# A four-layer transformer block in fp32 parts on one core: a reciprocal, three copies, key parts and an output product change places in the latent-attention layers

## What is computed

```python
h = x @ w_in
cq, ckv, k_rope, gate = split(h)              # 384, 256, 32 and 1024 columns
q  = (rmsnorm(cq, q_norm) @ w_q_up)           # 16 heads of 64 + 32
kv = (rmsnorm(ckv, kv_norm) @ w_kv_up)        # 16 heads of 64 (key) + 64 (value)
q_rope, k_rope = rope(q[..., 64:]), rope(k_rope)      # one rotary key for all heads
s = (q_full @ k_full.T) * scale; causal mask; p = softmax(s)
y = ((p @ v) * silu(gate)) @ w_out
x = layernorm(ALPHA * x + y)
```

## Time and profile before

| | us |
|---|---|
| median of three runs (1685.38 to 1687.06) | 1685.86 |
| the profiled execution's own time | 1687.21 |
| its span, first to last instruction | 1685.4 |
| TensorE busy | 1653.2 (98%) |
| VectorE busy | 775.5 (46%) |
| ScalarE busy | 768.0 (46%) |
| GpSimd busy | 657.7 (39%) |

### The profile page before, as it was taken

The page is one execution under the profiler, slowest core; times in us unless marked ns, Lnnn a source line. Parts: engine busy times, 40 slices in busy tenths (PEclk is TensorE's granted clock), DMA queues, the critical chain, the costliest instruction groups (busy, mean ns, idle before and its releaser), DMA issues.

```text
span 1685.4 us, 24539 instructions
## 1 busy us (share of the span) xinstructions
PE 1653.2 (98%) x9349; PEld 1344.0 (80%) x9349; DVE 775.5 (46%) x2038; ACT 768.0 (46%) x1565; POOL 657.7 (39%) x551
## 2 busy tenths in 40 slices
PE   8999999999999999999999999999999999999998
PEld 8777779777888787778777778777788888888877
DVE  2777636566343434336777636888142111001052
ACT  4566724566243535534566635336753222222252
POOL 4423224332243423234322224792154444444423
PEclk9999999999999999999999999999999999999999
DMA  6322144323442222153223145432153333333422
GB/s 171 70 45 73 50 160 133 78 65 61 153 146 76 78 62 79 47 176 108 62 45 84 47 154 143 129 88 76 41 171 102 100 93 95 100 100 88 125 63 88
DMA packets 216048, 161.19 MB, mean 96 GB/s; under 512 B 53755, under 2 KB 197147, under 8 KB 215932
## 3 DMA queue, kind: packets, MB, share of 16 engines
q1 hardware_dynamic: 205904, 130.21, 27.6%
q10 hardware_dynamic: 9804, 29.38, 5.6%
q0 software_dynamic: 224, 0.03, 0.1%
HBM read 148.32 MB, written 11.14 MB: 95 GB/s over the span
## 4 chain that ended last, share of the span: by engine, by line
PE 85%; DVE 6%; ACT 6%; issue 1%; POOL 1%; DMA 0%; ACTq 0%; DVEq 0%; SPq 0%; POOLq 0%
PE banks L481 23%; PE banks L483 22%; PE banks L482 22%; PE banks L740 5%; PE banks L701 4%; PE banks L755 4%; ACT AB L1487 1%; PE banks L906 1%; PE banks L724 1%; ACT w_hi L1357 1%; ACT G L1616 1%; DVE AB L2231 1%; ACT AB L1513 1%; PE banks L714 1%; POOL w_lo L2828 0%
## 5 line engine op out<-in xcount | busy, mean ns | idle before, releaser
L2828 POOL TENSOR_TENSOR w_lo<-w_raw,w_hi 128x512 fp32r<-128x512 f32 (+2 forms) x506 | 617.0, 1246 | 998.4 <-ACT w_hi L1357 987.2
L481 PE MATMUL banks<-XTh,w_hi 128*128 128x512 f32 (+5 forms) x1216 | 451.7, 371 | 2.6 <-DVE XTl L2290 1.4
L483 PE MATMUL banks<-XTh,w_lo 128*128 128x512 f32 (+5 forms) x1216 | 444.3, 365 | 0.0
L482 PE MATMUL banks<-XTl,w_hi 128*128 128x512 f32 (+5 forms) x1216 | 444.3, 365 | 0.0
L1357 ACT ACTIVATE w_hi<-w_raw 128x1024 fp32r<-128x1024 f32 (+4 forms) x254 | 250.3, 996 | 157.8 <-PE banks L483 106.4
L481 PEld LDWEIGHTS banks<-XTh,w_hi 128*128 128x128 f32 (+2 forms) x1216 | 228.1, 188 | 45.6 <-issue 5.2
L483 PEld LDWEIGHTS banks<-XTh,w_lo 128*128 128x128 f32 (+2 forms) x1216 | 228.0, 188 | 38.2
L482 PEld LDWEIGHTS banks<-XTl,w_hi 128*128 128x128 f32 (+2 forms) x1216 | 228.3, 188 | 37.2 <-issue 1.2
L481 PE MATMUL banks<-w_hi,OTh 128*128 128x512 f32 (+1 forms) x448 | 173.0, 386 | 0.6 <-DVE QKl L2055 0.5
L483 PE MATMUL banks<-w_hi,OTl 128*128 128x512 f32 (+1 forms) x448 | 167.9, 375 | 0.0
L482 PE MATMUL banks<-w_lo,OTh 128*128 128x512 f32 (+1 forms) x448 | 167.9, 375 | 0.0
(11 more groups left out here) (212 smaller groups left out, 2333.7 us busy)
## 6 DMA issues: line engine op xcount, KB each, us to landing
w_raw<-in_w_gate_up_dram SPq DMA_DIRECT2D x44, 512.0 KB, 3.8
w_raw<-in_fox_w_in_dram SPq DMA_DIRECT2D x30, 512.0 KB, 4.1
w_raw<-in_mla_w_in_dram SPq DMA_DIRECT2D x26, 512.0 KB, 4.7
w_raw<-in_w_in_dram SPq DMA_DIRECT2D x24, 512.0 KB, 3.9
w_raw<-in_w_down_dram SPq DMA_DIRECT2D x22, 512.0 KB, 3.5
w_raw<-in_swa_w_in_dram SPq DMA_DIRECT2D x20, 512.0 KB, 4.0
w_raw<-in_mla_w_out_dram SPq DMA_DIRECT2D x16, 512.0 KB, 3.7
x_spill<-AB ACTq DMA_DIRECT2D x16, 512.0 KB, 2.6
```

Of the source, the lines that this page charges most:

```text
L481: nc.tensor.matmul(o, ah, bh, start=first, stop=False, skip_group_check=True)
L482: nc.tensor.matmul(o, ah, bl, start=False, stop=False, skip_group_check=True)
L483: return nc.tensor.matmul(o, al, bh, start=False, stop=last, skip_group_check=True)
L2828: ins = pool.tensor_tensor(low[at], raw[at], high[at].bitcast(F32), ALU.subtract)
```

## The change

The two latent layers, and in them the opening and rounds 1 and 3, are reordered on VectorE and ScalarE. TensorE's order and the instructions themselves stay.

- Opening, VectorE: the reciprocal for latents 3 and 4 moves ahead of the low parts of latents 0 to 2 (it stood behind gate 0). The three copies of the rotary key's low part move from ahead of those low parts to behind `rope_sum`, ahead of the low part of key tile 0.
- Rounds 1 and 3, ScalarE: the query's high part moves ahead of unit B, that of key 0 ahead of unit C, and that of key 1 ahead of the last exponential of head 1 (`fill(i - 1, 7)` inside `exps`).
- Rounds 1 and 3, VectorE: key 1's low part moves ahead of the norm of head 0, and the gated output product ahead of maxima 2 (`mixed_first`).

```diff
@@ exps (ScalarE)
                     for t in range(T):
+                        if x == 1 and t == T - 1:
+                            fill(i - 1, 7)
                         sc = pr.score(b, x, t)
@@ fill of a latent layer (ScalarE)
-                        if pos == 5:
+                        if pos == 5 and i < 0:
                             rope(g)
                             query(i + 3)
-                            if i > 0:
-                                keys(g, 0)
+                        elif pos == 5:
+                            rope(g)
+                            hi(QKh[:, 3 + (i + 3) % 2, :], group()[:, :])
+                            advance()
+                            hi(QKh[:, 2 * g % 3, :], group()[:, :])
+                            advance()
+                        elif pos == 7 and i > 0:
+                            keys(g, 1)
...
                         elif pos == 2:
-                            keys(g, 1)
+                            if i < 0:
+                                keys(g, 1)
                             rotated(g)
@@ mixed (VectorE)
                         src = otmp[:, :]
+                    if i in mixed_first:
+                        maxima(i + 2, 2)
                     fill(i, 3)
@@ rounds (VectorE)
                     fill(i, 2)
-                    maxima(i + 2, 2)
+                    if i not in mixed_first:
+                        maxima(i + 2, 2)
@@ opening (VectorE)
                 lo(QKl[0:ROPE, 7, :], RA[0:ROPE, :], QKh[0:ROPE, 7, :]).then_inc(kr_done, 1)
-                dve.wait_ge(kr_done, 7 * j + 4)
-                for n in range(1, 4):
-                    nc.vector.tensor_copy(QKl[ROPE * n:ROPE * n + ROPE, 7, :], QKl[0:ROPE, 7, :].bitcast(F32)).then_inc(kr_done, 1)
+                c.g += 1
+                inverse_root(1, c.g)
                 for i in range(3):
                     low_latent(i)
-                c.g += 1
-                root_at = c.g
                 gate(0)
                 gate_at[0] = c.g
-                inverse_root(1, root_at)
                 scaled(1, 3, 5)
@@ fill(-2, 0) (VectorE)
                             rope_sum()
+                            dve.wait_ge(kr_done, 7 * j + 4)
+                            for n in range(1, 4):
+                                nc.vector.tensor_copy(QKl[ROPE * n:ROPE * n + ROPE, 7, :],
+                                                      QKl[0:ROPE, 7, :].bitcast(F32)).then_inc(kr_done, 1)
                             keys(0, 0)
@@ fill, pos 4 and 2 (VectorE)
                             rope_sum()
+                            if i > 0:
+                                keys(g, 1)
...
                             if i < 0:
                                 keys(g, 0)
-                            keys(g, 1)
+                                keys(g, 1)
                             rope_high(g)
@@ call
-                pair_attention(mla_pairs(), fill, norm_last=(1, 3))
+                pair_attention(mla_pairs(), fill, norm_last=(1, 3), mixed_first=(1, 3))
```

More of the change, by code:

```diff
@@ L2179, in _, with pair_attention @@
             gate_at = {}
-            def pair_attention(pairs, fill, norm_last=()):
+            def pair_attention(pairs, fill, norm_last=(), mixed_first=(), norm_split=None):
                 a0, n_pairs = c.pair, len(pairs)
```

## The result

| | before | changed |
|---|---|---|
| median of ten runs each | 1685.90 (1685.38 to 1688.81) | 1689.85 (1688.56 to 1691.70) |
| profiled execution, own time | 1687.21 | 1689.22 |
| its span | 1685.4 | 1687.4 |

What follows compares the result with a forecast made beforehand. TensorE, busy 98% of the span, was taken as the bound. Openings 2 x -0.45, rounds 1 2 x +0.2 and rounds 3 2 x +0.6 sum to +0.7 us: 1686.6 us from 1685.86, range 1683.7 to 1688.5.

Steps and rivals of the forecast that it cites:

- Forecast +0.2 and +0.6: Second head's transposes: TensorE loses 0.2 us in each round 1 and 0.6 us in each round 3.
- costs nothing of its own: Rounds 1 and 3, VectorE: output product ahead of the maxima adds no cost; its start was put at 131.81, today 131.61.
- the slack of 1.01 and 0.81: Rounds 1 and 3: us between the second norm's end and TensorE's first transpose of the second head, absorbing VectorE lateness.
- 0.45 us gained in each opening: Opening, first value tile: net gain after the moved copies and a charge for GpSimd; bounds 0 and 1.5 us.
- the 1.45 us wait goes: Opening, query 0: TensorE's wait for gate 1's bank vanishes with the reciprocal moved ahead, 1.45 us.
- some 0.2 us: Opening, rotary sum and moved copies: charge for GpSimd working beside them, 0.2 us.
- half a microsecond before TensorE wants its bank: Opening, VectorE: gate 1 ends at 61.6, ahead of query 0's possible start at 62.13.
- Nothing later in the layer should give it back or take it: After the opening: its gain stays unchanged, as some 5 us of tiles precede the scores reading the copied key.
- C: Opening: copies blocked by GpSimd wait some 0.7 us, opening gives nothing, rounds cost 1.6: 1687.5 us, chance 19%.
- D: Odd rounds: VectorE's chain is later than reckoned, waiting for key 1's high part ahead of the norm: 1689.0 us, chance 10%.
- A: Rounds 1 and 3: lateness fits the slack, each of four rounds keeps its 0.41 us: 1683.4 us, chance 20%.
- B: Openings: copies are hidden as well, -1.45 us each, rounds -1.6 in all: 1681.4 us, chance 6%.

Runs made afterwards that it cites:

- rounds_only: Kernel before with only the change's reordering of rounds 1 and 3, opening as before: 1688.74 us, ratio 1.0018.
- r_key1: Kernel before with only key 1's high and low parts moved early in rounds 1 and 3, weight roundings and maxima as before: 1688.3 us, one run.
- open_swap: Kernel before with the change's opening, plus ScalarE's rounding of the key-and-value weight moved behind gate 1's tanh: 1692.88 us, ratio 1.0027.
- best3: Changed kernel with rotary copies directly behind the reciprocal, key 1 behind the norm, unit C behind key 1's high part: 1685.11 us, ratio 0.9996 to before.
- best: Changed kernel with rotary copies behind both key low parts and key 1 behind the norm, C ahead of the exponentials: 1684.58 us, ratio 0.9993 to before.

## Why the prediction was wrong

**The bound and the method held.** TensorE's idle time was the only thing that moved, at the places named: the gate's wait, the first value tile, the second key tile, the second head's transposes, and at one that was not named, the end of the second latent layer.

**The rounds held.** Forecast +0.2 and +0.6; measured +0.24 and +0.6, repeated within 0.02 and shown alone by `rounds_only`. VectorE's idle time was put at 1.2 to 1.4 and came to 1.08 and 1.61. In round 3 the gain at the key tile was there (-0.42) and was lost with 0.6 on top. One part of the reasoning was off and cancelled: I let the chain pass to TensorE at the transposes alone and wrote that the output product "costs nothing of its own". It was there that most of the loss fell (0.75 of 1.02 in round 3). The sum is the same since both hang on one late chain. `r_key1`, with the product behind the maxima, shows that the slack of 1.01 and 0.81 is not the one that decides in that order: an idle time under it still cost 0.67. That much the prediction had said itself ("without this part the key wait would have hit it too").

**The opening failed, by size and so by sign.** The failed step is the term "0.45 us gained in each opening" (measured: 0.64 and 0.71 lost), and within it "the 1.45 us wait goes" (0.95 of it went, and the first query tile still waited 0.34 us for the gate, the sign that the prediction had named for a wrong first step) and the charge of "some 0.2 us" for GpSimd. Three durations were taken over from places where they were undisturbed:

- *The products.* I let gate 1 end at 61.6, "half a microsecond before TensorE wants its bank". The two products took 3.20 instead of 1.42, so the query gained 0.95 and not 1.45, and the rotary sum came 0.49 later than reckoned. `open_swap` shows the cause: with GpSimd's pieces elsewhere they take 1.41 and the query gains 1.45.
- *The sum.* I let the copies follow it after 0.61, the distance of undisturbed neighbours; it took 0.92 as before and the copies started 0.96 behind its start: 0.35 more.
- *The copies.* 1.75 in place of 1.32: 0.43 more.

I had charged 0.2 for the latter two. 0.49 + 0.35 + 0.43 - 0.2 is 1.07, and what was missing is 0.64 + 0.45 = 1.09. In both openings it comes to 2.3 us.

**A second term was put at nothing.** "Nothing later in the layer should give it back or take it" had a reason for the copied key alone. At the end of the second latent layer the changed kernel lost 0.47 and, profiled again, 0.25 us, as did every kernel with the reciprocal ahead, by 0.25 to 1.23. With the openings' 2.3 and the 0.7 forecast that makes the 3.5 of the steps. What links the reciprocal to that end stays open.

**The bounds were the real fault.** I gave the opening a worst case of 0. The trace of before held what was needed: the reciprocal of the earlier trace rows at 58.04 stood where GpSimd had two pieces of 512 columns, from 58.34 on. I had drawn on GpSimd's timeline only beside the copies' new place. I asked what the moved instruction would meet in its new place, and not what would move into its old one.

**The rivals.** C had the right mechanism and too small a price: it let a copy wait once and the opening come out at nothing. D gave 1689.0, nearest to the time, for another reason: its further lateness in the rounds didn't happen, and that it came nearest was luck. A and B fell, since the slack was used up and the copies' full length was on the path.

The mechanism of the opening was that of a rule I had cited: the Trainium skill, "SBUF — State Buffer", section "SBUF: two separate sides", names as takers of the shared lock, beside the copies, VectorE instructions with two SBUF inputs while GpSimd reads SBUF too. By that the products, the latent low parts and the rotary sum were to be suspected as much as the copies; I had applied the rule to the sum and the copies only. The traces agree for products (1.41 and 3.20), latent low parts (1.29 and 3.06) and copies (1.32 and up to 1.90). They agree in the other direction too: the reciprocal, with one input, takes 3.35 beside GpSimd and 3.33 without it. In these traces it is the second comer that waits: a GpSimd piece of 256 columns takes 0.73 us at 64.92 in the kernel before and 1.20 at 66.03, where a sum of two SBUF tensors (L2446) had started 0.09 earlier and took its undisturbed 0.69.

## What to carry to other kernels

When an instruction moves, price two places: what it will meet where it goes, and what slides into the slot that it leaves. A long instruction with one input, like this reciprocal, may be sheltering its neighbours from GpSimd's work. And a slack belongs to the first consumer that is late: list all that hang on a chain before taking one consumer's slack as the limit.

## What the runs showed that was not expected

- *VectorE beside GpSimd.* Two products 1.41 to 3.20; two latent low parts 1.29 to 3.06; two rotary low parts on 32 rows 1.38 to 2.50; three copies 1.32 to 1.75 or 1.90; the rotary sum 0.68 to 0.92 in the opening and to 0.98 in the second layer's rounds; the reciprocal unchanged. Of such a group it is one or two instructions that wait (the two rotary low parts took 0.69 and 1.80). Each other order put another group of instructions beside GpSimd's pieces (`open_swap`, `best3`, `best`); none of those tried was free of it.
- *The clock.* Stretches of 3.4 us at half clock came in some traces and not in others, and where the offsets show them in full each cost 1.5 to 1.6 us, as much as any step here. In `open_swap` one followed each of the two waits of 2.51 us. In the kernel before one followed a wait of 0.99 at 1032.66; six of the fourteen traces have one there, the changed kernel had the same wait and none, so the length of the wait alone doesn't decide it.
- *A weight's landing.* The wait for one transfer at the end of the second latent layer was 2.31 to 2.42 us in seven traces and 2.77 to 3.76 in the seven with the reciprocal ahead, 200 us away from it. An edit can cost time where none of its instructions are; two traces of the changed kernel alone (0.47 and 0.25) would have passed for scatter, and only the fourteen together show the split.
